# Merging two mixer branches and projecting out in one stage of 512-token blocks, with paired filter spectra and two DMA queues in the long convolutions

## Chip, cores and metric

The kernel runs on one core of one Trainium2 chip. The metric is the device time of one execution in microseconds (us); lower is better. Arithmetic is in float32; large products are split into a rounded high part and the rest (`hi`, `lo`), and three TensorE matmuls make one exact enough product. Engines are named as in the profile: PE (TensorE matmuls), PEld (its weight loads), DVE (VectorE), ACT (ScalarE), POOL (GpSimd), SP (SyncE).

## The reference

One layer over 2048 latent tokens and 256 context tokens of width 1024. After a modulated norm and one input projection, a Mamba-2 branch gives `y_m`, and a Hyena branch gives `y_h` by two rounds of long convolutions. What the changed stages compute is this, with the convolution done by FFT of 4096 points:

```
def bidir_long_conv(u, h_fwd, h_bwd):
    k = jnp.concatenate([h_fwd[:1] + h_bwd[:1], h_fwd[1:], jnp.zeros_like(h_fwd[:1]), jnp.flip(h_bwd[1:], axis=0)], axis=0)
    u_f, k_f = jnp.fft.rfft(u, n=2 * seqlen, axis=1), jnp.fft.rfft(k, n=2 * seqlen, axis=0)
    return jnp.fft.irfft(u_f * k_f[None], n=2 * seqlen, axis=1)[:, :seqlen]

for o, gate in enumerate((x1, x2)):                      # hyena_mixer
    z = gate * (bidir_long_conv(z, filt[:, 0, o], filt[:, 1, o]) + h_bias[o] * z)

ym = gated_group_rmsnorm(y_m, m_z, m_norm_w)             # mixer_output
yh = y_h * silu(h_gate)
merged = sigmoid(g_m) * (ym @ w_branch_m) + sigmoid(g_h) * (yh @ w_branch_h)
x = x + gate * (merged @ w_out)                          # gate: 1024 values from c, then a final rmsnorm
```

## The kernel before

The program is a row of phases, each a block in which every engine runs its own list of instructions, written out by hand and tied by semaphores. Nothing crosses from one phase into the next. Between phases, tensors lie in HBM, channels in rows and tokens in columns (`u_s`, `z2_s`, `hg_s`, `g_s`, `ym_s`, `mix_s`). The profile cuts digits off names, so `z2_s` reads `z_s` there.

**Long convolutions** (`phase_long_convs`, tiles `conv_...`). Four blocks of 256 channels, two orders each, are eight convolutions, in the order of the list `convs`. One convolution has a forward transform (`first`, from the tile `x`), then 32 planes: a matmul `forward`, DVE's product `prod` with the plane of the filter's spectrum (`spec`, 256 KB, L1078), two matmuls `inverse` (L995, L996). Then come `turn` (L963) and `last` (L973), and DVE multiplies by the gate `gin` into `x` (L1056), in four chunks of two products. PE does the transform of the next convolution and the turn of this one in one loop. All DMAs of the phase are on SP in one list: the spectra of a plane in two halves (L908, L910), through four slots; three gate chunks at planes 24, 26 and 28; at plane 4 after an order-1 convolution the store of `z2_s`, at plane 20 a new `x` (L890). SP works them off in this order, and a wait in one holds all behind it.

**Step sizes** (`phase_step_sizes`, `dt_...`) among other things computes the 1024 values of the output gate, repeated over 128 partitions, as 16 matmuls of 512 columns (L1128).

**Merge** (`phase_merge`, `mg_...`). Eight blocks of 256 tokens. Both branches' weights (16 slabs of 512 KB, one for each 128 output channels) are loaded once, split by ACT (high part) and by POOL and DVE in turn (low part), and stay. For each block and branch PE makes eight output tiles of 24 matmuls. DVE multiplies a tile by its gate, POOL adds the two branches, ACT stores to `mix_s`. The Mamba branch comes first, its group norm (squares, sums over partitions by PE, root, reciprocal) is done a block ahead.

**Output** (`phase_output`, `out_...`). `w_out` is loaded, scaled by the gate (DVE, L2066), split by ACT and POOL. Then come 16 tiles of 128 tokens: `mix_s` is loaded back and split, PE makes 2 by 24 matmuls of 512 columns with the tokens in rows, DVE adds the residual, and the norm and the store follow.

## Time and profile before

| | |
|---|---|
| time, 3 runs | 4273.19, 4275.51 (median), 4277.01 us |
| profiled execution | 4276.4 us, span 4274.6 us |
| mean granted clock of TensorE | 0.938 of full speed |
| busy | PE 3708.5, DVE 1663.0, ACT 1162.1, POOL 915.8 us |
| long convolutions | about 2224 to 2967 us of the span |
| merge and output | 3603 us to the end |

Busy time is a share of the whole span; each stage has its own limit, so the windows and the waits of a stage say more than the totals. PE's busy time includes matmuls that run at the lower clock. A wait is put down to what came last.

### The profile page before, as it was taken

Reading aid. Unit: us, or ns where it says so; the run is one execution under the profiler, and the core shown is the slowest. Engines: PE = TensorE matmul, PEld = TensorE weight load, DVE = VectorE, ACT = ScalarE, POOL = GpSimd, SP = SyncE. Lnnn points to the kernel's source line nnn. Section 1 sums busy time; section 2 is a strip of 40 time slices with the busy share of each in tenths; the row PEclk is TensorE's granted clock in tenths of the full one; section 3 lists DMA queues with packets and bytes.
Section 4 is the critical chain, followed back from the end, with each engine's and each line's share of the span. In section 5 each row is a group of like instructions: output and inputs, shape, how many; then the busy total and the mean of one; then the engine's idle time right before and its main releaser. Section 6 shows DMA issues by size and latency. Waiting matters only on the chain. (4 is left out here: it accounts for less than half of the span.)

```text
span 4274.6 us, 49330 instructions
## 1 busy us (share of the span) xinstructions
PE 3708.5 (87%) x18426; PEld 3067.7 (72%) x18426; DVE 1663.0 (39%) x1979; ACT 1162.1 (27%) x2308; POOL 915.8 (21%) x449
## 2 busy tenths in 40 slices
PE   6599999999999999967989978996456886799879
PEld 2588888888888888846977766764445775699867
DVE  6600443004333400045435443443176765455332
ACT  4311111111011111123764433442103552211022
POOL 0311222112222222110000000000056662433241
PEclk8799999999999999988999999998688998899989
DMA  6411111111111111179995665445785443443343
GB/s 244 154 59 74 70 67 69 74 74 73 64 69 74 74 74 74 54 283 298 293 247 140 146 143 138 114 122 156 256 307 200 155 159 128 148 137 128 110 141 123
DMA packets 595897, 588.97 MB, mean 138 GB/s; under 512 B 285627, under 2 KB 534619, under 8 KB 583387
## 3 DMA queue, kind: packets, MB, share of 16 engines
q1 hardware_dynamic: 515853, 421.13, 33.7%
q10 hardware_dynamic: 79920, 166.22, 10.0%
q8 instruction: 74, 1.21, 0.1%
q14 instruction: 50, 0.41, 0.0%
HBM read 375.84 MB, written 211.42 MB: 137 GB/s over the span
## 5 line engine op out<-in xcount | busy, mean ns | idle before, releaser
L563 PE MATMUL pl_bank<-hl_hi,pl_w_hi 128*128 128x512 f32 x2336 | 923.0, 395 | 17.1 <-POOL pl_w_lo L548 17.1
L564 PE MATMUL pl_bank<-hl_lo,pl_w_hi 128*128 128x512 f32 x2336 | 922.6, 395 | 0.0
L565 PE MATMUL pl_bank<-hl_hi,pl_w_lo 128*128 128x512 f32 x2336 | 922.6, 395 | 0.0
L563 PEld LDWEIGHTS pl_bank<-hl_hi,pl_w_hi 128*128 128x128 f32 x2336 | 440.8, 189 | 120.0 <-issue 17.3
L565 PEld LDWEIGHTS pl_bank<-hl_hi,pl_w_lo 128*128 128x128 f32 x2336 | 440.8, 189 | 103.1
L564 PEld LDWEIGHTS pl_bank<-hl_lo,pl_w_hi 128*128 128x128 f32 x2336 | 440.9, 189 | 102.9
L622 DVE TENSOR_SCALAR pl_acc<-pl_raw,pl_taps 128x2048 f32<-128x2048 f32 x40 | 83.8, 2094 | 930.2 <-ACT pl_raw L587 930.2
L545 POOL TENSOR_TENSOR pl_w_hi<-pl_w,pl_zero 128x1024 fp32r<-128x1024 f32 x73 | 138.3, 1894 | 1246.2 <-PE pl_bank L565 1242.0
L1338 POOL TENSOR_TENSOR st_faded<-st_state,ssd_whole 128x1024 f32<-128x1024 f32 x36 | 82.7, 2306 | 1209.0 <-DVE st_state L1365 1153.0
L1078 DVE TENSOR_TENSOR conv_prod<-conv_bank,conv_spec 128x512 f32<-128x512 f32 x256 | 175.3, 690 | 246.8 <-DMA conv_spec<-spec_s 208.1
L587 ACT ACTIVATE pl_raw<-pl_bank 128x512 f32<-128x512 f32 x160 | 91.7, 598 | 630.5 <-PE pl_bank L565 383.4
L587 ACT ACTIVATE pl_res<-pl_bank 128x512 f32<-128x512 f32 x132 | 78.9, 599 | 633.6 <-PE pl_bank L565 632.9
L1044 ACT COPY conv_v<-conv_bank 128x256 f32<-128x256 f32 x256 | 154.1, 602 | 310.0 <-PE conv_bank L996 310.0
L995 PE MATMUL conv_bank<-conv_prod,tab_wi 128*128 128x256 f32 x512 | 167.0, 409 | 77.3 <-DVE conv_prod L1078 76.5
L548 POOL TENSOR_TENSOR pl_w_lo<-pl_w,pl_w_hi 128x1024 fp32r<-128x1024 f32 x73 | 209.7, 2873 | 5.7
L1762 PE MATMUL mg_bank<-mg_m_hi,mg_w_hi 128*128 128x256 f32 x512 | 146.6, 286 | 44.5 <-DVE mg_mix L1927 27.4
L995 PEld LDWEIGHTS conv_bank<-conv_prod,tab_wi 128*128 128x128 f32 x512 | 96.8, 199 | 110.1 <-DVE conv_prod L1078 97.7
L624 DVE SCALAR_TENSOR_TENSOR pl_acc<-pl_raw,pl_taps,pl_acc 128x2048 f32<-128x2048 f32 x40 | 170.6, 4266 | 5.7 <-DVE pl_acc L622 0.2
L996 PE MATMUL conv_bank<-conv_prod,tab_wj 128*128 128x256 f32 x512 | 160.4, 396 | 0.0
L824 DVE COPY spec_y<-spec_bank 64x256 f32<-64x256 f32 x256 | 109.4, 427 | 124.0 <-PE spec_bank L798 121.9
L985 PE MATMUL conv_bank<-conv_y,tab_wf 128*128 128x256 f32 x512 | 154.1, 388 | 1.1 <-DVE conv_y L1018 1.1
L798 PEld LDWEIGHTS spec_bank<-tab_fk,spec_xin 128*128 128x128 f32 x1024 | 134.4, 195 | 25.2 <-DMA spec_xin<-kern_s 19.5
(224 smaller groups left out, 6748.3 us busy)
## 6 DMA issues: line engine op xcount, KB each, us to landing
conv_spec<-spec_s SPq DMA_DIRECT2D x504, 128.0 KB, 2.9
pl_w<-in_w_rec SPq DMA_DIRECT2D x73, 512.0 KB, 3.4
kern_s<-taps_res SPq DMA_DIRECT2D x16, 2048.0 KB, 7.0
spec_xin<-kern_s SPq DMA_DIRECT2D x64, 512.0 KB, 5.4
spec_s<-spec_res ACTq DMA_DIRECT2D x128, 256.0 KB, 3.9
st_xb<-tok_s SPq DMA_DIRECT2D x36, 768.0 KB, 6.9
u_s<-pl_res ACTq DMA_DIRECT2D x24, 1024.0 KB, 3.8
xbc_s<-pl_res ACTq DMA_DIRECT2D x16, 1024.0 KB, 3.8
```

What stands on the lines that cost most here:

```text
L548: nc.gpsimd.tensor_tensor(w_lo[:, q, :], w[:, q, 0:D], w_hi[:, q, :].bitcast(F32), ALU.subtract).then_inc(s_lo, 1)
L563: pe.matmul(out, w_hi[:, q, m], h_hi[:, k, r], start=(k == 0), stop=False)
L564: pe.matmul(out, w_hi[:, q, m], h_lo[:, k, r], start=False, stop=False)
L565: mm = pe.matmul(out, w_lo[:, q, m], h_hi[:, k, r], start=False, stop=(k == KT - 1))
L587: nc.scalar.activation(dst, bank[b][:, 0:BW], func).then_inc(s_ev, 1)
L624: nc.vector.scalar_tensor_tensor(out=acc[:], in0=raw[:, q, 0:T], scalar=w0, in1=acc[:], op0=ALU.mult, op1=ALU.add).then_inc(s_tap, 1)
L985: pe.matmul(bank[ubank[k % 4]][:, 0:CB], wf[:, k, :], y[:, k, :], start=True, stop=True).then_inc(s_u, 1)
L995: pe.matmul(out, wi[:, k, :], prod[:, n % 4, 0, :], start=True, stop=False)
L996: pe.matmul(out, wj[:, k, :], prod[:, n % 4, 1, :], start=False, stop=True).then_inc(s_v, 1)
L1044: nc.scalar.copy(v[:, :, k], bank[2 + k % 2][:, 0:CB]).then_inc(s_vm, 1)
L1078: nc.vector.tensor_tensor(prod[:, n % 4], bank[ubank[k % 4]][:, None, 0:CB].to_broadcast([P, 2, CB]), spec[:, n % SLOT], ALU.mult).then_in ...
L1762: pe.matmul(o, w_hi[:, n, m], hi[:, k, :], start=(k == 0), stop=False)
```

## The change

Four things change.

1. The long convolutions' spectra are loaded in pairs of planes: 256 KB a transfer, four slots of two planes. SP issues nothing else. The loads of `x` and of the gates and the stores of `z2_s` go to POOL's queue, in a list of their own, the store in four chunks.
2. The output gate is computed as one column for each 128 channels (`keep["gcol"]`), not repeated over partitions.
3. Merge and output become one phase (`phase_merge_output`, tiles `mo_...`) over four blocks of 512 tokens. In each block three branches of eight tiles follow: H (Hyena), M (Mamba), O (output projection). Each tile has 24 matmuls of 512 columns with channels in rows. The weight slab of every tile is loaded and split anew, through three slots. The scaling by the gate and the residual come after the O tile (`yT`); then PE turns `yT` by transposes into tokens in rows (`tok`, a single tile of two banks), four turns a block, each followed by the final norm and the store.
4. `mix_s` and the phase boundary between the two are gone.

In what follows a line of "..." stands where lines of the diff are left out, among them most that it removes; those are in the functions printed above.

```diff
-        spec = ph.sb("spec", [P, SLOT, 2, CB])
+        spec = ph.sb("spec", [P, SLOT, 2, 2, CB])
...
+            for j, (blk, o) in enumerate(convs):
+                for h in range(NPL // 2):
+                    n = NPL // 2 * j + h
+                    if n >= SLOT:
+                        sp.wait_ge(s_p, 2 * (n - SLOT) + 2)
+                    s = spec_v[o * NBK + blk, h]
+                    to = spec[:, n % SLOT].rearrange("p k a n -> p (k a) n")
+                    sem = s_k[n % SLOT]
+                    sp.dma_start(to[0:NA], s).then_inc(sem, 16)
+                    if h:
+                        sp.dma_start(to[NA:P], s).then_inc(sem, 16)
+                    else:
+                        sp.dma_start(to[NA + 1:P], s[1:NA]).then_inc(sem, 16)
+                        sp.dma_start(to[NA:NA + 1, 0], s[0:1, 1]).then_inc(sem, 16)
+                        sp.dma_start(to[NA:NA + 1, 1:4], s[0:1, 1:4]).then_inc(sem, 16)
+        @block.gpsimd
+        def _(pool):
+            def load_x(blk, c):
+                pool.dma_start(x[:, blk % 2, 16 * c:16 * (c + 1), :], u_v[0][blk, :, 16 * c:16 * (c + 1), :]
+                               ).then_inc(s_x[blk % 2][c], 16)
             def load_gate(j, c):
                 n = 4 * j + c
                 if n >= 3:
-                    sp.wait_ge(s_gate, 2 * (n - 3) + 2)
...
+                    pool.wait_ge(s_gate, 2 * (n - 3) + 2)
+                pool.dma_start(gin[:, n % 3], u_v[1 + convs[j][1]][convs[j][0], :, 16 * c:16 * (c + 1), :]
+                               ).then_inc(s_g[n % 3], 16)
+            for blk in range(2):
+                for c in range(4):
+                    load_x(blk, c)
+            for j, (blk, o) in enumerate(convs):
+                if o == 1:
+                    for c in range(4):
+                        load_gate(j, c)
+                    for c in range(4):
+                        pool.wait_ge(s_gate, 8 * j + 2 * c + 2)
+                        pool.dma_start(z2_v[blk, :, 16 * c:16 * (c + 1), :], x[:, blk % 2, 16 * c:16 * (c + 1), :]
+                                       ).then_inc(s_st, 16)
+                    if blk < 2:
+                        pool.wait_ge(s_st, 64 * (blk + 1))
+                        for c in range(4):
+                            load_x(blk + 2, c)
                 else:
...
+                    for c in range(4):
+                        load_gate(j, c)
+            pool.wait_ge(s_st, 256)
...
                         dve.wait_ge(s_u, n + 1)
-                        dve.wait_ge(s_k[n % SLOT], 32 * (n // SLOT + 1) + (32 * (j + 1) if k % SLOT == 0 else 0))
+                        if k % 2 == 0:
+                            h = n // 2
+                            dve.wait_ge(s_k[h % SLOT], 32 * (h // SLOT + 1) + (32 * (j + 1) if h % SLOT == 0 else 0))
...
-                                                spec[:, n % SLOT], ALU.mult).then_inc(s_p, 1)
+                                                spec[:, n // 2 % SLOT, k % 2], ALU.mult).then_inc(s_p, 1)
...
+            for m in range(KT):
+                if m % 4 == 0:
+                    pe.wait_ge(s_aw[m // 4], 16)
                 for k in range(KT):
+                    mm = pe.matmul(sums[4][:, 2 * m:2 * m + 2], aw[:, m // 4, k, m % 4 * P:(m % 4 + 1) * P],
+                                   keep["silu"][:, k, :], start=(k == 0), stop=(k == KT - 1))
+            mm.then_inc(s_gate, 1)
...
+def phase_merge_output(nc, t, keep, ym_s, z2_s, hg_s, gates_s, out):
+    BW = 512
     NB = SEQ // BW
+    NS = 3 * KT * NB
+    H, M, O = 0, 1, 2
+    par = keep["par"]
     with ExitStack() as ctx:
...
+        w = ph.sb("w", [P, 3, D])
+        w_hi, w_lo = ph.sb("w_hi", [P, 3, D], F32R), ph.sb("w_lo", [P, 3, D], F32R)
+        hi, lo = ph.sb("hi", [P, 2, KT, BW], F32R), ph.sb("lo", [P, 2, KT, BW], F32R)
+        zin = ph.sb("zin", [P, 2, 2, BW])
...
+        item = lambda b, br, k: KT * (3 * b + br) + k
+        def steps():
+            for b in range(NB):
+                for br in range(3):
+                    for j in range(KT):
+                        yield item(b, br, j), b, br, j
+        def rest(b, j):
+            if b:
+                return [j]
+            return [] if j < 4 else [2 * j - 8, 2 * j - 7]
         @block.sync
         def _(sp):
+            def load_w(s):
+                if s >= 3:
+                    sp.wait_ge(s_wlo, s - 2)
+                sp.dma_start(w[:, s % 3, :], t["w_br"][s % (3 * KT)]).then_inc(s_w[s % 3], 16)
+            def load_z(b, k):
+                n = KT * b + k
+                if n >= 2:
+                    sp.wait_ge(s_lo, item((n - 2) // KT, H, (n - 2) % KT) + 1)
+                sp.dma_start(zin[:, n % 2, 0, :], z2_v[:, k, cols(b)]).then_inc(s_z[n % 2], 16)
+                sp.dma_start(zin[:, n % 2, 1, :], hg_v[:, k, cols(b)]).then_inc(s_z[n % 2], 16)
+            def load_g(b, br, k):
+                n = 2 * KT * b + KT * br + k
+                if n >= 4:
+                    m = n - 4
+                    sp.wait_ge(s_ev, item(m // (2 * KT), m // KT % 2, m % KT) + 1)
+                sp.dma_start(gin[:, n % 4, :], g_v[1 - br, :, k, cols(b)]).then_inc(s_g[n % 4], 16)
+            def load_x(b, k):
+                n = KT * b + k
+                if n >= 4:
+                    sp.wait_ge(s_ev, item((n - 4) // KT, O, (n - 4) % KT) + 1)
+                sp.dma_start(xin[:, n % 4, :], x_v[:, k, cols(b)]).then_inc(s_x[n % 4], 16)
+            def load_ym(b):
+                if b:
+                    sp.wait_ge(s_lo, item(b - 1, M, KT - 1) + 1)
+                for a in range(4):
+                    sp.dma_start(ym[:, 2 * a:2 * a + 2], ym_v[:, 2 * a:2 * a + 2, cols(b)]).then_inc(s_ym[a], 16)
+            load_z(0, 0)
+            load_w(0)
+            load_z(0, 1)
+            load_w(1)
+            for k in range(2, KT):
+                load_z(0, k)
+            load_w(2)
+            load_ym(0)
+            sp.dma_start(ident[:], t["ident"]).then_inc(s_fw, 16)
+            sp.dma_start(fw[:], t["final_norm_w"].to_broadcast([P, D])).then_inc(s_fw, 16)
+            load_g(0, H, 0)
+            load_g(0, H, 1)
+            for s, b, br, j in steps():
+                if br == M and j == 0 and b + 1 < NB:
+                    load_ym(b + 1)
+                if s + 3 < NS:
+                    load_w(s + 3)
+                if s + 2 < NS:
+                    b2, br2, j2 = (s + 2) // (3 * KT), (s + 2) // KT % 3, (s + 2) % KT
+                    if br2 == O:
+                        load_x(b2, j2)
+                        if b2 + 1 < NB:
+                            load_z(b2 + 1, j2)
+                    else:
+                        load_g(b2, br2, j2)
...
+            def low(s):
+                pool.wait_ge(s_whi, s + 1)
+                nc.gpsimd.tensor_tensor(w_lo[:, s % 3, :], w[:, s % 3, :], w_hi[:, s % 3, :].bitcast(F32),
                                         ALU.subtract).then_inc(s_wlo, 1)
...
         @block.tensor
         def _(pe):
+            def tile(s, b, br, j):
+                pe.wait_ge(s_wlo, s + 1)
+                if s >= 4:
+                    pe.wait_ge(s_ev, s - 3)
+                q, slot = s % 3, (3 * b + br) % 2
+                for k in range(KT):
+                    if j == 0:
+                        pe.wait_ge(s_lo, item(b, br, k) + 1)
+                    m = slice(k * P, (k + 1) * P)
+                    pe.matmul(bank[s % 4][:], w_hi[:, q, m], hi[:, slot, k, :], start=(k == 0), stop=False)
+                    pe.matmul(bank[s % 4][:], w_hi[:, q, m], lo[:, slot, k, :], start=False, stop=False)
+                    mm = pe.matmul(bank[s % 4][:], w_lo[:, q, m], hi[:, slot, k, :], start=False, stop=(k == KT - 1))
                 mm.then_inc(s_mm, 1)
...
+            def turn(b, q):
+                n = 4 * b + q
+                pe.wait_ge(s_ev, item(b, O, KT - 1) + 1)
+                if n:
+                    pe.wait_ge(s_res, n)
+                for k in range(KT):
+                    mm = pe.transpose(tok[:, k // 4, k % 4 * P:(k % 4 + 1) * P], yT[:, k, q * P:(q + 1) * P], ident[:])
+                mm.then_inc(s_t, 1)
+            pe.wait_ge(s_one, 1)
+            pe.wait_ge(s_fw, 32)
+            for s, b, br, j in steps():
+                tile(s, b, br, j)
+                if b == 0 and br == H and j in (0, 1):
+                    sums(0, 2 * j)
+                    sums(0, 2 * j + 1)
+                if br == O and j in (1, 2) and b + 1 < NB:
+                    sums(b + 1, 2 * j - 2)
+                    sums(b + 1, 2 * j - 1)
+                if br == H and b and 1 <= j <= 4:
+                    turn(b - 1, j - 1)
+            for q in range(4):
+                turn(NB - 1, q)
         @block.scalar
         def _(act):
+            def weights(s):
+                act.wait_ge(s_w[s % 3], 16 * (s // 3 + 1))
+                if s >= 3:
+                    act.wait_ge(s_mm, s - 2)
+                nc.scalar.activation(w_hi[:, s % 3, :], w[:, s % 3, :], ACT.Copy).then_inc(s_whi, 1)
...
+            for s, b, br, j in steps():
+                if br == H:
+                    if b == 0 and j in (1, 2):
+                        mean(0, 2 * j - 2)
+                        mean(0, 2 * j - 1)
+                    if b and 2 <= j <= 5:
+                        finish(b - 1, j - 2)
+                    for k in rest(b, j):
+                        if b == 0 and k % 2 == 0:
+                            inverse(0, k // 2)
+                        m_value(b, k)
+                    gates(s, b, br, j, mixed[:, j, :]).then_inc(s_ev, 1)
+                    for k in rest(b, j):
+                        low(b, M, k)
+                elif br == M:
+                    gates(s, b, br, j, part[:, j % 2, :]).then_inc(s_ev, 1)
+                    if j:
+                        low(b, O, j - 1)
+                    dve.wait_ge(s_ev, s + 1)
+                    nc.vector.tensor_tensor(mixed[:, j, :], mixed[:, j, :], part[:, j % 2, :], ALU.add).then_inc(s_val, 1)
+                    if j == KT - 1:
+                        low(b, O, j)
+                else:
+                    if b + 1 < NB:
+                        if j in (2, 3):
+                            mean(b + 1, 2 * j - 4)
+                            mean(b + 1, 2 * j - 3)
+                        if j >= 4:
+                            inverse(b + 1, j - 4)
+                        h_value(b + 1, j)
+                    n = KT * b + j
+                    dve.wait_ge(s_mm, s + 1)
+                    dve.wait_ge(s_x[n % 4], 16 * (n // 4 + 1))
+                    if b and j == 0:
+                        dve.wait_ge(s_t, 4 * b)
+                    nc.vector.scalar_tensor_tensor(out=yT[:, j, :], in0=bank[s % 4][:], scalar=keep["gcol"][:, j:j + 1],
+                                                   in1=xin[:, n % 4, :], op0=ALU.mult, op1=ALU.add).then_inc(s_ev, 1)
+                    if b + 1 < NB:
+                        low(b + 1, H, j)
+            for q in range(4):
+                finish(NB - 1, q)
```

How the lists of DMAs change, at three places. The first is SP in the middle of the first convolution: planes from the 24th on, before.

```order
L908 DMA conv_spec<-spec_s 64x2x256
L910 DMA conv_spec<-spec_s 64x2x256
L897 DMA conv_gin<-u_s 128x16x64
L908 DMA conv_spec<-spec_s 64x2x256
L910 DMA conv_spec<-spec_s 64x2x256
```

The same queue of the changed kernel, at the stage's start (the first two planes have small transfers of their own):

```order
L896 DMA conv_spec<-spec_s 64x4x256
L900 DMA conv_spec<-spec_s 63x4x256
L901 DMA conv_spec<-spec_s 1x256
L902 DMA conv_spec<-spec_s 1x3x256
L896 DMA conv_spec<-spec_s 64x4x256
L898 DMA conv_spec<-spec_s 64x4x256
```

No gate load stands between spectra now; the pair of halves covers two planes. The second place is POOL's queue in the same stage, which had no instruction there before. This is its whole list; `x4` is four in a row.

```order
L907 DMA conv_x<-u_s 128x16x64 x8
L914 DMA conv_gin<-u_s 128x16x64 x12
L926 DMA z2_s<-conv_x 128x16x64 x4
L907 DMA conv_x<-u_s 128x16x64 x4
L914 DMA conv_gin<-u_s 128x16x64 x4
L926 DMA z2_s<-conv_x 128x16x64 x4
L907 DMA conv_x<-u_s 128x16x64 x4
L914 DMA conv_gin<-u_s 128x16x64 x12
L926 DMA z2_s<-conv_x 128x16x64 x4
L914 DMA conv_gin<-u_s 128x16x64 x4
L926 DMA z2_s<-conv_x 128x16x64 x4
```

All 64 transfers of `x`, gates and `z2_s` moved here; after the third and the fourth convolution the stores and the loads of a new `x` stand ahead of the next gates. The third place is SP at the start of the last stage. Before, in the merge:

```order
L1690 DMA mg_ym<-ym_s 128x4x256 x2
L1708 DMA mg_mix<-in_w_br 128x1024 x2
L1694 DMA mg_z2<-z2_s 128x4x256 x2
L1699 DMA mg_hg<-hg_s 128x2x256 x2
L1708 DMA mg_gates<-in_w_br 128x1024 x2
```

Now, behind seven pairs of `zin` loads (the last of them is shown), which are two deep:

```order
L1705 DMA mo_zin<-z2_s 128x512
L1706 DMA mo_zin<-hg_s 128x512
L1699 DMA mo_w<-in_w_br 128x1024
L1725 DMA mo_ym<-ym_s 128x2x512 x4
L1735 DMA mo_ident<-in_ident 128x128
L1736 DMA mo_fw<-in_final_norm_w 128x1024
L1713 DMA mo_gin<-g_s 128x512 x2
L1699 DMA mo_w<-in_w_br 128x1024
```

The branch that is computed first is the other one, so `ym` moved behind `z2_s`; the identity and the norm weights, which only the end of a block needs, are waited for by PE ahead of its first tile.

## Rows read from the trace of the kernel before

**Rows 1.** Windows of four stages: PE, PEld, DVE, ACT, POOL busy; clock; DMA share; GB/s.

```profile
2228.00:2957.00 729.00, 645.23 (x2816) 496.24 (x2816) 328.20 (x576) 318.89 (x640) 0.00 (x0) 0.96 0.57 135
...
3638.00:4050.00 412.00, 383.96 (x3128) 382.07 (x3128) 200.11 (x252) 72.17 (x106) 143.59 (x115) 0.96 0.40 130
...
4050.00:4090.00 40.00, 0.34 (x1) 0.35 (x2) 22.14 (x8) 10.35 (x10) 27.79 (x11) 0.55 0.54 184
...
4090.00:4267.00 177.00, 176.52 (x768) 145.54 (x767) 42.80 (x61) 35.15 (x59) 35.34 (x15) 0.99 0.38 128
```

**Rows 2.** The waits from 2228 to 2957: us, times, longest.

```profile
DVE conv_prod L1078 <- DMA conv_spec<-spec_s: 208.1, 170, 11.1
...
PE conv_bank L995 <- DVE conv_prod L1078: 76.5, 30, 8.8
```

**Rows 3.** The timeline of the first convolution, SP and PE: start, us, what.

```profile
2223.96 16.11 SPq L890 DMA_DIRECT2D conv_x<-u_s  x8
...
2228.21 4.34 PE L951 MATMUL conv_bank<-tab_fx,conv_x 128*128 128x256 f32 x12 [10.54 <-DMA conv_x<-u_s]
...
2247.80 1.53 PE L985 MATMUL conv_bank<-conv_y,tab_wf 128*128 128x256 f32 x6 [1.05 <-DVE conv_y L1018]
...
2277.74 1.61 SPq L908 DMA_DIRECT2D conv_spec<-spec_s  x1
```

**Rows 4.** The timeline of PE after the first z2 store.

```profile
2513.89 1.22 PE L995 MATMUL conv_bank<-conv_prod,tab_wi 128*128 128x256 f32 x2 [8.19 <-DVE conv_prod L1078]
```

**Rows 5.** The waits from 3602 to 4275.

```profile
PE mg_bank L1762 <- DVE mg_mix L1927: 27.4, 1, 27.4
...
PE out_bank L2023 <- POOL out_m_lo L2007: 40.3, 1, 40.3
```

**Rows 6.** The line of the x loads: issue ns, min/median/max, and landing.

```profile
L890 SPq DMA_DIRECT2D conv_x<-u_s x16: 372/2186/3646, 2224.0 to 2637.5; - x16
...
DMA to landing us min/median/max: 4.2/7.5/8.9
```

**Rows 7.** The timeline of DVE, first gate product of convolutions 0 and 1.

```profile
2303.83 0.69 DVE L1056 TENSOR_TENSOR conv_x<-conv_bank,conv_gin 128x512 f32<-128x512 f32 x1 [1.36 <-PE conv_bank L973]
...
2386.57 0.69 DVE L1056 TENSOR_TENSOR conv_x<-conv_bank,conv_gin 128x512 f32<-128x512 f32 x1 [1.36 <-PE conv_bank L973]
```

**Rows 8.** The timeline of PE in the step sizes, the output gate.

```profile
2982.32 15.59 PE L1128 MATMUL dt_sum<-dt_aw,dt_silu_rep 128*128 128x512 f32 x32 [7.50 <-DMA dt_aw<-in_ada_w]
```

**Rows 9.** The timeline of PE, four transposes.

```profile
2298.80 0.60 PE L963 MATMUL conv_bank<-tab_ident,conv_v 128*128 128x128 f32 x4
```

**Rows 10.** The windows of the projection and the output, 100 us each.

```profile
500.00:600.00 100.00, 100.00 (x432) 81.05 (x432) 42.09 (x15) 19.21 (x22) 23.58 (x9) 1.00 0.18 69
...
4120.00:4220.00 100.00, 100.00 (x443) 82.81 (x442) 25.42 (x36) 22.75 (x37) 23.21 (x10) 1.00 0.44 147
```

**Rows 11.** The groups of the merge: busy us, mean ns.

```profile
L1884 DVE RECIPROCAL mg_ms<-mg_ms 128x1024 f32<-128x1024 f32 x8 | 52.3, 6543 | 1.1 <-ACT mg_ms L1790 1.1
...
L1809 ACT ACTIVATE mg_w_hi<-mg_gates 128x1024 fp32r<-128x1024 f32 x8 | 8.3, 1054 | 2.9 <-DMA mg_gates<-in_w_br 2.9
...
L1853 POOL TENSOR_TENSOR mg_w_lo<-mg_gates,mg_w_hi 128x1024 fp32r<-128x1024 f32 x4 | 11.4, 2845 | 3.5 <-ACT mg_w_hi L1809 3.5
```

**Rows 12.** The timeline of the merge's start, SP and PE.

```profile
3607.47 0.92 SPq L1690 DMA_DIRECT2D mg_ym<-ym_s  x2
...
3637.96 0.58 PE L1762 MATMUL mg_bank<-mg_m_hi,mg_w_hi 128*128 128x256 f32 x1 [17.04 <-POOL mg_w_lo L1853]
```

**Rows 13.** The timeline of the end.

```profile
4266.56 1.22 DVE L2071 TENSOR_TENSOR out_y<-out_x,out_bank 128x1024 f32<-128x1024 f32 x1 [6.53 <-PE out_bank L2025]
...
4270.93 0.35 ACTq L2049 DMA_DIRECT2D out<-out_res  x1
```

**Rows 14.** The windows with gate loads and of the transforms behind.

```profile
2283.00:2289.00 6.00, 3.03 (x12) 2.12 (x12) 2.07 (x3) 1.20 (x2) 0.00 (x0) 1.00 1.18 227
...
2300.00:2310.00 10.00, 10.00 (x50) 7.30 (x49) 5.65 (x12) 6.49 (x16) 0.00 (x0) 1.00 0.01 2
```

More of the change, by code:

```diff
@@ L1974, in phase_output @@
-        block = ctx.enter_context(nc.Block())
-        def tiles(eng, body):
-            with eng.Fori(0, NT // 2) as i:
-                for q in range(2):
-                    body(2 * i + q, i, q)
+        ones, ident = ph.sb("ones", [P, P]), ph.sb("ident", [P, P])
+        bank = [ph.ps(f"bank{i}", [P, BW]) for i in range(4)]
+        ssq = [ph.ps(f"ssq{i}", [P, BW]) for i in range(2)]
+        tok = ph.ps("tok", [P, 2, BW])
+        s_w, s_whi, s_wlo, s_mm, s_ev = ph.sems("w", 3), ph.sem("whi"), ph.sem("wlo"), ph.sem("mm"), ph.sem("ev")
@@ new lines, in phase_merge_output @@
+        s_val, s_hi, s_lo, s_part = ph.sem("val"), ph.sem("hi_done"), ph.sem("lo_done"), ph.sem("part_done")
+        s_ym, s_z, s_g, s_x = ph.sems("ym_in", 4), ph.sems("z_in", 2), ph.sems("g_in", 4), ph.sems("x_in", 4)
+        s_sq, s_add, s_ss, s_ms, s_root, s_rec = (ph.sem(n) for n in ("sq_done", "add", "ss_done", "ms_done", "root", "rec"))
+        s_one, s_t, s_sq2, s_ms2, s_root2, s_rec2, s_res = (ph.sem(n) for n in (
+            "one", "turn", "sq2", "ms2", "root2", "rec2", "res_done"))
@@ new lines, in sums @@
+            def sums(b, g):
+                n = GROUPS * b + g
+                pe.wait_ge(s_add, n + 1)
+                if n >= 2:
+                    pe.wait_ge(s_ms, n - 1)
+                pe.matmul(ssq[g % 2][:], ones[:], ms[:, g, :], start=True, stop=True).then_inc(s_ss, 1)
+            def turn(b, q):
[6 more added lines that the diff above has]
+                mm.then_inc(s_t, 1)
@@ new lines, in store @@
+            def store(b, q):
+                n = 4 * b + q
+                act.wait_ge(s_res, n + 1)
+                act.dma_start(out[n * P:(n + 1) * P, :], res[:, n % 2, :]).then_inc(s_st[n % 2], 16)
+            for k in range(KT):
+                high(0, H, k)
+                if k in (1, 3):
+                    weights(k // 2)
+            for k in range(KT):
+                square(0, k)
+            for s, b, br, j in steps():
+                if s + 2 < NS:
+                    weights(s + 2)
+                if br == H:
+                    if b == 0 and j == 3:
+                        root(0)
+                    if b and 2 <= j <= 5:
+                        norm(b - 1, j - 2)
+                    for k in rest(b, j):
+                        high(b, M, k)
+                    if b and 3 <= j <= 6:
+                        store(b - 1, j - 3)
+                elif br == M:
+                    high(b, O, j)
+                    if b + 1 < NB:
+                        square(b + 1, j)
+                elif b + 1 < NB:
+                    if j == 4:
+                        root(b + 1)
+                    high(b + 1, H, j)
```

541 lines of the change are left out of this document (117 added, 424 removed).

## The prediction

> **What bounds the kernel now.** I read it stage by stage, because the change touches three stages and leaves the others alone. The busy times by window come first [rows 1]: in the long convolutions PE is busy for 645 of 729 us, in the merge for 384 of 412, between merge and output for 0.3 of 40, in the output for 176.5 of 177. So PE sets the pace wherever it has work, and what can be won is its idle time or its own instructions.
>
> The waits of the convolution stage [rows 2] say whose idle time it is: DVE's product with the spectra waits 208 us for the spectra's DMA, and PE's inverse transform waits 76.5 us in 30 pieces for DVE. The reader should see that these are one stall, and that the queue's order makes it. SP holds gate loads, the z2 store and x loads between the spectra: a spectrum behind a gate load took 1.61 us to issue [rows 3], and PE stood still for 8.19 us after the z2 store [rows 4].
>
> In the last two stages PE idles twice: 27.4 us while the second branch's weights are loaded and split, and 40.3 us while the output weights are scaled and split [rows 5].
>
> The sum is made against the profiled execution, 4276.4 us (span 4274.6 and 1.8 around it); the median of the runs is 4275.5, 0.9 lower. Less than 0.2% (8.6 us) cannot be told from no change.
>
> **Long convolutions, what goes.** SP keeps only spectra, in pairs: half as many issues of 256 KB instead of 128 KB. At worst a pair's two transfers cost twice what one spectrum's did, and the pace is as now; at best half. Taken away is the order: -76.5 us [rows 2].
>
> **Long convolutions, what comes.** All 64 transfers of x, gates and z2 (512 KB each, in rows of 256 bytes) go to POOL, which issues no DMA in the trace of before. So the time G from one to the next on POOL is unknown, and much hangs on it. From below, SP issued eight of the same transfers in 16.11 us [rows 3], 2.0 each; I take 2.2, the median of one issue [rows 6]. From above, 8.9 us, the slowest landing of one [rows 6]: then nothing overlaps. No row is near enough to choose by; I take the middle, G = 5.5.
>
> Start: now the first x load is issued at 2223.96, PE starts at 2228.21 and has used four chunks at 2247.80: 23.8 us, 4.9 a chunk [rows 3]. After it the fourth chunk lands at 4G + 2.2 (the quickest landing of 4.2 less 2.0 of issue [rows 6]) and takes 4.9: 29.1 us with G = 5.5, so +5. With 2.2: 0. With 8.9: +19.
>
> Period: where convolutions 2 and 3 end, POOL does in order, from the first product of a gate to the gate that the next convolution needs first: a gate load, four stores, a wait of about 5 us for their landing, four x loads, a gate load, and its landing of about 4: 10G + 9. From one convolution's first product to the next one's are 82.7 us [rows 7], about 78 without stalls. So up to G = 6.9 this costs nothing; beyond it, 10 us for each us of G, twice.
>
> Contention: after each of those two convolutions eight transfers (17.6 us at 2.2) run beside the spectra, which are eight planes ahead in their four pair slots. A plane lasts about 1.3 us of the stage (the period less its transform), so 10.3 us are covered; 7.3 is the most each can cost, 0 the least, since the DMA engines have a mean share of 0.57 here [rows 1]. I take 4 each: +8.
>
> End: the last stores follow one another at G, and one z2 store of 2 MB goes: -4 with 2.2, +4 with 5.5, +20 with 8.9.
>
> Sum: -76.5 + 5 + 8 + 4 = -60 (from -80 to +10).
>
> **Step sizes.** The output gate is computed as 64 matmuls of two columns instead of 16 of 512. Now these are 32 records in 15.6 us [rows 8]. After it they are 128 records, bound by their weight loads. Four 128x128 transposes, each with its own load, took 0.60 [rows 9], 0.15 each; half of that is my lower bound. 128 by 0.075 to 0.15 is 10 to 19 us. With a smaller copy behind it I take -3 (-6 to +3).
>
> **Merge and output.** PE's busy time now is 384.0 + 176.5 = 560.5 us [rows 1], 3072 matmuls of 256 columns, 768 of 512 and 28 sums of squares. After it there are 2304 of 512 columns. Their pitch is 0.2257 by the output stage (443 in 100 us) and 0.2315 by the projection (432), whose operands have the roles of the new ones [rows 10]; 0.229 gives 527.6 (520 to 533). The sums become 16 of 512 columns, at most 0.97 each by [rows 8]: 15. So -18.
>
> Both stalls go: -67.7 [rows 5], since weights are streamed, one slab of 512 KB for each output tile of 24 by 0.229 = 5.5 us. What hides it: ACT's half of the split takes 1.06 and POOL's 2.8 [rows 11], and they start two tiles ahead, when PE frees the slot: about 4.2 of 11 us. Without that cover each us over is paid in every one of 96 tiles.
>
> Sixteen turns of eight transposes come, at 0.11 to 0.15 each [rows 9]; twelve turns lie between tiles: +12.
>
> Start: now PE begins at 3637.96, 30.5 us after SP's first issue at 3607.47 [rows 12]. After it PE's first tile waits for the identity and the norm weights. SP issues them behind z loads that wait two by two for DVE's low parts (three round trips of about 6 us), a weight slab and 2 MB of ym (about 15 us with landing): 33.5, so +3.5.
>
> Block borders: in each of the last four tiles of O, DVE has a reciprocal of 3.27 (half of 6.54 [rows 11]) and three 512-wide operations of 0.69 (as those of [rows 7]): 5.34 us in a tile of 5.5, and it starts late behind ACT's root. The last low part comes some 3 us after the tile; PE wants it 4.8 us into the next. And with 2 MB of ym ahead of it in SP's queue, the fourth slab of branch M arrives about when it is wanted. Nothing to 25 us; I take +15, the slow clock of the first matmuls included.
>
> Tail: now 4266.56 to the end, 8.0 us [rows 13]. The four last turns share one PSUM tile, so each goes through turn, square, root, reciprocal and product before the next: 4270.93 - 4267.78 = 3.1 and the turn's 1.1, 4.2 by four, +0.7 ahead, 3.7 for the last store: 21. So +13.
>
> Sum: -18 - 67.7 + 12 + 3.5 + 15 + 13 = -42.
>
> **Total.** -60 - 3 - 42 = -105: 4171 us in the profiled execution, 4170.5 by the median; I say 4171. Its own range is 4145 (G = 2.2, a pitch of 0.2257) to 4200 (G = 6.9, late borders): chance 0.52.
>
> **Rivals.** First, POOL issues in 7 to 10 us. At 8.9: start +19, end +20, period 2 by 10 by 2.0 = +40, contention +8, against -76.5: +10. 4276 + 10 - 3 - 42 = 4241. For it speaks that no row has POOL issue at all, against it nothing but the same. 0.18.
>
> Second, slower than before: the same mechanism beyond its turning point. Each us beyond 8.9 costs 20 + 4 + 5 = 29, and 35 are left, so G = 10.1 decides. At G = 12 the time is 4330. The place is the convolution stage alone, PE waiting for gates and x. 0.15.
>
> Third, the spectra wait for the DMA engines and not for the queue's order. In a stretch with gate loads the share of the DMA engines is 1.18, in the transforms behind it 0.01 [rows 14]: full where PE waits. That the gates move to where it is 0.01 speaks for the gain; but x loads and stores still fall on the spectra, and their stalls of 8.2 at four places would stay: 33 of the 76.5. The stage then gives -27, and the time is 4204. The Trainium skill ("DMA: Bandwidth & Descriptors", section "Issuing engines are not separate DMA queues") says that starting transfers from several engines saves only the time of starting them, since the same 16 DMA engines carry all. The share of 1.18 agrees; by the rule alone it would be 4204. 0.08.
>
> Fourth, the new last stage is bound by its streams. 27 MB for each block of 132 us is 207 GB/s, and 238 in the tiles of O, against 130 in the merge now [rows 1]. Should the DMA engines give only 200, each of the 24 O tiles with loads for a next block takes 1.05 us longer, and late slabs double that: +25 to +50, about 4208. 0.07.
>
> **How the numbers follow.** Prediction 4171. The range is 4146 to 4280: 0.05 lies below (G at its lower bound and the rest good), 0.13 above (G over 10). Faster by over 0.2%: 0.52 + 0.18 + 0.08 + 0.07, less a little at the turning point: 0.83. Within 0.2%: 0.02. Slower: 0.15.
>
> **What would show it.** The spacing of POOL's issues in the convolutions: under 6.9 right, above it the price by the formula. PE's waits for the product with the spectra under 20 us in total. In the last stage: 3.5 us more to the first matmul, about 565 us to the last one, 21 behind it. A PE stall at the fourth tile of M or the first of H would be the borders, a stall in every tile the weights' split. What would make the prediction wrong above all is G.

## The result

The changed kernel takes 4172.9 us (median of 4 runs, 4165.82 to 4183.68), the kernel before 4274.8 in the same job (4273.19 to 4277.01): a ratio of 0.9764, 95% interval 0.9750 to 0.9779. 4171 was forecast. The profiled execution is the slowest of the four, 4183.7 us (span 4181.9); the stages below are read from it.

A stage is measured from its first DMA issue to that of the next; with the same code the changed convolutions took 676.3 to 683.2 us in six profiles, the changed last stage 615.9 to 619.3 in seven. These are the issues in the profile of the kernel before that don't stand ahead of the prediction ([rows 3, 12] have the other two):

```profile
2966.64 0.34 SPq L1106 DMA_DIRECT2D dt_raw<-dt_c  x1
...
3004.89 1.18 SPq L1234 DMA_DIRECT2D tok_in<-xbc_c  x2
```

And of the changed kernel, from the timelines of POOL and SP:

```profile
2231.60 9.32 POOL L907 DMA_DIRECT2D conv_x<-u_s  x8 [270.57 <-POOLq L63]
2242.95 1.15 POOL L914 DMA_DIRECT2D conv_gin<-u_s  x1 [2.03 <-issue]
...
2231.03 0.61 SPq L896 DMA_DIRECT2D conv_spec<-spec_s  x1
...
2910.68 0.33 SPq L1107 DMA_DIRECT2D dt_raw<-dt_c  x1
...
2961.43 1.16 SPq L1232 DMA_DIRECT2D tok_in<-xbc_c  x2
...
3562.72 0.34 SPq L1705 DMA_DIRECT2D mo_zin<-z_s  x1
```

| stage, us | before | after | change | forecast |
|---|---|---|---|---|
| up to the convolutions (not changed) | 2224.0 | 2231.0 | +7.1 | 0 |
| long convolutions | 742.7 | 679.6 | -63.1 | -60 |
| step sizes | 38.2 | 50.8 | +12.5 | -3 |
| the stages between (not changed) | 602.6 | 601.3 | -1.3 | 0 |
| merge and output | 667.1 | 619.2 | -47.9 | -42 |
| span | 4274.6 | 4181.9 | -92.7 | -105 |

The first row is no effect of the change. The projection, the same code in both, made 4305 matmuls from 500 to 1500 us in one profile and 4287 in the other, at a granted clock of 1.00 in both (last section).

The windows of the changed kernel, with the columns of [rows 1]: the convolutions, a pass over planes, a transform, the stretch after the first z2 stores, the output gate's matmuls, the last stage:

```profile
2238.89:2903.92 665.03, 630.82 (x2816) 493.95 (x2816) 327.18 (x576) 318.79 (x640) 65.21 (x57) 0.97 0.66 149
2345.00:2387.00 42.00, 42.00 (x200) 36.60 (x199) 21.24 (x33) 21.25 (x37) 0.00 (x0) 1.00 0.84 211
2318.00:2343.00 25.00, 24.91 (x112) 17.13 (x111) 14.14 (x29) 12.90 (x30) 3.81 (x4) 1.00 0.26 64
2501.00:2518.00 17.00, 13.42 (x63) 11.47 (x61) 5.53 (x8) 6.62 (x11) 8.00 (x7) 1.00 1.09 227
2924.00:2952.00 28.00, 27.45 (x129) 27.45 (x129) 8.95 (x14) 1.81 (x2) 0.00 (x0) 0.50 0.13 48
3600.00:4158.00 558.00, 552.94 (x2432) 450.88 (x2432) 328.15 (x340) 185.05 (x247) 249.03 (x107) 0.99 0.53 177
```

Read the last three columns (clock, share of the DMA engines, GB/s; the profile's share can come out over 1). A pass moves 211 GB/s, and by the view of DMA queues from 2345 to 2387 nearly all of it is SP's, that is spectra, 8.39 MB or 200 GB/s; POOL's 0.44 MB are the end of a gate load (packets, MB, share):

```profile
q1 hardware_dynamic: 8701, 8.39, 80.2%
q0 software_dynamic: 123, 0.44, 3.8%
```

A transform moves 64 GB/s, and where POOL's seven transfers (four of x, three of gates) come on top of a pass the engines are full at 227. The fifth line of the windows is the loser: PE is busy for 27.45 of 28 us, at half the clock. The waits of the convolution stage and the longest piece, beside those of [rows 2, 4], with a shorter piece behind it and the window in which the longest ends:

```profile
DVE conv_prod L1081 <- DMA conv_spec<-spec_s: 40.7, 13, 11.5
...
PE conv_bank L996 <- DVE conv_prod L1081: 30.9, 6, 9.1
...
2523.52 1.22 PE L996 MATMUL conv_bank<-conv_prod,tab_wi 128*128 128x256 f32 x2 [9.10 <-DVE conv_prod L1081]
...
2531.48 0.70 PE L996 MATMUL conv_bank<-conv_prod,tab_wi 128*128 128x256 f32 x2 [2.47 <-DVE conv_prod L1081]
...
2523.50:2526.00 2.50, 2.48 (x6) 2.03 (x7) 0.56 (x1) 0.36 (x1) 0.00 (x0) 0.50 1.07 238
```

76.5 us in 30 pieces became 30.9 in 6. PE's busy time for the same 2816 records fell as well, from 645.2 to 630.8. Behind the stall of 9.1 us the granted clock is 0.50 and a pair of matmuls takes 1.22 us; behind the one of 2.47 us it takes 0.70. There are fewer long stalls now, and the mean clock of the stage is 0.97 instead of 0.96.

Last, PE's timeline in the step sizes, at the start of the last stage and in the tail, which answers to [rows 8, 12, 13]:

```profile
2924.55 27.47 PE L1128 MATMUL dt_sum<-keep_silu,dt_aw 128*128 128x2 f32 x128 [5.09 <-DMA dt_aw<-in_ada_w]
...
3600.10 0.77 PE L1787 MATMUL mo_bank<-mo_hi,mo_w_hi 128*128 128x512 f32 x1 [42.72 <-DMA mo_fw<-in_final_norm_w]
...
4157.17 0.39 PE L1789 MATMUL mo_bank<-mo_hi,mo_w_lo 128*128 128x512 f32 x1
4158.40 1.09 PE L1805 MATMUL mo_tok<-mo_ident,mo_yT 128*128 128x128 f32 x8 [0.85 <-DVE mo_yT L1989]
4162.73 1.94 PE L1805 MATMUL mo_tok<-mo_ident,mo_yT 128*128 128x128 f32 x8 [3.24 <-DVE mo_res L1947]
```

### The profile page after: what moved, and what is told of

Read it like the earlier page. It is cut to its first block and busy times, and to the rows that moved or that the text cites. A ratio compares the mean times of both kernels' runs of the same rounds, so it can differ in the third digit from the quotient of the medians.

```text
span 4181.9 us, 45508 instructions
## 1 busy us (share of the span) xinstructions
PE 3715.1 (89%) x17082; PEld 3012.0 (72%) x17082; DVE 1723.6 (41%) x2008; ACT 1233.9 (30%) x2392; POOL 1033.8 (25%) x482
## 5 line engine op out<-in xcount | busy, mean ns | idle before, releaser
L1787 PE MATMUL mo_bank<-mo_hi,mo_w_hi 128*128 128x512 f32 x768 | 305.4, 398 | 47.2 <-DMA mo_fw<-in_final_norm_w 42.7
L1759 POOL TENSOR_TENSOR mo_w_lo<-mo_w,mo_w_hi 128x1024 fp32r<-128x1024 f32 x96 | 237.5, 2477 | 293.2 <-ACT mo_w_hi L1829 293.2
L1789 PE MATMUL mo_bank<-mo_hi,mo_w_lo 128*128 128x512 f32 x768 | 300.6, 391 | 0.0
L1788 PE MATMUL mo_bank<-mo_lo,mo_w_hi 128*128 128x512 f32 x768 | 300.6, 391 | 0.0
L1787 PEld LDWEIGHTS mo_bank<-mo_hi,mo_w_hi 128*128 128x128 f32 x768 | 145.2, 189 | 81.3 <-issue 45.0
L996 PE MATMUL conv_bank<-conv_prod,tab_wi 128*128 128x256 f32 x512 | 159.6, 394 | 31.5 <-DVE conv_prod L1081 30.9
L1788 PEld LDWEIGHTS mo_bank<-mo_lo,mo_w_hi 128*128 128x128 f32 x768 | 145.3, 189 | 31.6 <-issue 1.9
L1789 PEld LDWEIGHTS mo_bank<-mo_hi,mo_w_lo 128*128 128x128 f32 x768 | 145.0, 189 | 30.3
```

The costliest lines, as they stand in the source:

```text
L996: pe.matmul(out, wi[:, k, :], prod[:, n % 4, 0, :], start=True, stop=False)
L1759: nc.gpsimd.tensor_tensor(w_lo[:, s % 3, :], w[:, s % 3, :], w_hi[:, s % 3, :].bitcast(F32), ALU.subtract).then_inc(s_wlo, 1)
L1787: pe.matmul(bank[s % 4][:], w_hi[:, q, m], hi[:, slot, k, :], start=(k == 0), stop=False)
L1788: pe.matmul(bank[s % 4][:], w_hi[:, q, m], lo[:, slot, k, :], start=False, stop=False)
L1789: mm = pe.matmul(bank[s % 4][:], w_lo[:, q, m], hi[:, slot, k, :], start=False, stop=(k == KT - 1))
```

## The experiments

The first four take the convolution stage apart, the next four the step sizes and the two ends of the last stage; the last two follow from them. Stage lengths are from one profile each. Four kernels (the two output gates, the late wait, the tail) were run once, beside a run of 4285.1 us of the kernel before; since the runs of one kernel differ by up to 18 us, these four are read by their stages and not by their totals.

**The convolutions alone.** `phase_long_convs` of the changed kernel in the kernel before.

> The kernel before with the changed long convolutions alone (paired spectra on SP; x, gates and z2 on POOL). In the two profiles the stage from its first DMA issue to the first issue of the step sizes went from 742.7 us to 679.6. If the stages are independent, the stage here is again 680 (+-2) and the whole time is 63 below before, 4212 us (ratio 0.985), the other stages as before. Rival: a part of the 102 us comes from how the stages act on each other (clock, transfers that run over a border); then the whole moves by less than 55 or more than 71.

4211.4 us, ratio 0.985 (0.9829 to 0.9871); stage 683.2, the step sizes 38.6, the last stage 665.8. The stage is 1.2 us over the 682 that the expectation allowed, and the longest of the six profiles with the same code. Within that spread the stages are independent.

**Two queues with single planes.**

```diff
-                for h in range(NPL // 2):
+                for k in range(NPL):
+                    load_spec(j, k)
```

`load_spec` is that of the kernel before, on SP; everything else stays on POOL.

> The changed kernel, but the spectra are loaded plane by plane (128 KB an issue, four slots of one plane), SP still holding nothing else and POOL the rest. Theory order of the queue: what was won is that spectra no longer queue behind gates, x and z2, so nearly all of the 63 us stays: convolution stage 680 to 690 us. Rival issue time: SP needs 1.30 us for the two issues of a plane and PE 1.29 for a plane, so with single planes nothing can be caught up and the four slots cover half as much; then the stage goes back to 710 to 740 us.

Ratio 0.9828 (0.9804 to 0.9852), stage 699.9: between the two expectations.

**Pairs in one queue.**

```diff
         def _(sp):
...
+                    if k % 2 == 0:
+                        load_pair(j, k // 2)
+                    if j >= 1 and k == 4 and convs[j - 1][1] == 1:
...
```

Behind it z2, x and gates follow in SP's list as in the kernel before.

> The changed kernel, but x, gates and z2 stand in SP's list at their old places again, between paired spectra. Theory order of the queue: the stalls behind them come back, the stage is 725 to 745 us. Rival issue time: halved issues and slots twice as deep absorb a gate load of 0.6 to 1.7 us, only the z2 stores and x loads still stall (five stalls of 8 us); then the stage is 690 to 710 us.

Ratio 0.9857 (0.9837 to 0.9876), stage 718.0, again between the two expectations. PE's waits with single planes in two queues, and with pairs in one:

```profile
PE conv_bank L1000 <- DVE conv_prod L1083: 42.9, 18, 5.9
```

```profile
PE conv_bank L996 <- DVE conv_prod L1081: 58.4, 19, 7.3
```

From 742.7 us the pairs alone win 24.7, the second queue alone 42.8, both 63.1. Both theories hold for a part: the queue's order is the greater one, and the pairs are the other, on top of it. Which of the two things that pairs bring does it, slots twice as deep or half the issues, was not taken apart.

**The loads spread over the pass.**

```diff
+            def at(j, k):
+                pool.wait_ge(s_p, NPL * j + k)
...
                         for c in range(4):
+                            at(j + 1, 2 + 4 * c)
                             load_x(blk + 2, c)
```

The second x at the start and the first gate loads of a pass wait for planes in the same way.

> The changed kernel, but POOL's second x load at the start, and the x and first gate loads after the z2 stores, wait for the 2nd, 6th, 10th ... plane of the pass that they run beside (a wait for DVE's products, no byte more or less). PE's waits for the product are 30.9 us in 6 pieces now, each behind such a burst of up to 7 transfers of 512 KB. Theory burst: the DMA engines are full for the 17 us that a burst needs, spread over a pass of 42 us it fits beside the spectra; waits under 8 us, stage 645 to 655 us, the whole 25 to 33 us faster than the changed kernel. Rival: spectra are late for another reason (slots, SP's issues being slow by themselves); then the waits stay above 20 us and the stage at 672 to 680.

```profile
PE conv_bank L1006 <- DVE conv_prod L1091: 35.0, 13, 5.9
```

A miss. The waits broke into 13 shorter pieces and did not shrink; the stage is 685.0, no shorter, and the ratio 0.9769 (0.9747 to 0.9792), that of the changed kernel. So it is not the burst. What I had not looked at is the second line of the windows: the spectra alone take about 200 GB/s where 227 were moved with the engines full.

**The output gate with 128 columns.**

```diff
-                    mm = pe.matmul(sums[4][:, 2 * m:2 * m + 2], aw[...],
-                                   keep["silu"][:, k, :], ...)
+                    mm = pe.matmul(sums[4 + m // 4][:, m % 4 * P:(m % 4 + 1) * P], aw[...],
+                                   silu_rep[:, k, :], ...)
```

> The changed kernel, but the 64 matmuls of the output gate move 128 equal columns instead of 2 (same weights, same order, 64 times the columns). Now they take 27.5 us for 128 records (0.215 each) at a granted clock of 0.50 all the way; before, 32 records of 512 columns took 15.6 us at 0.89. Theory clock: matmuls of two columns never brought the clock up; with 128 columns it rises within a few us and the block takes 15 to 20 us. Rival weight loads: 128 loads of 128x128 in float32 cost 0.21 us each whatever is moved; then the block takes 27 us or more at a higher clock, or 0.50 stays.

4163.4 us in one run; window and timeline:

```profile
2918.00:2935.00 17.00, 16.36 (x129) 16.35 (x130) 8.96 (x14) 3.18 (x3) 0.00 (x0) 0.87 0.28 104
...
2918.64 16.29 PE L1131 MATMUL dt_sum<-dt_silu_rep,dt_aw 128*128 128x128 f32 x128 [3.79 <-DMA dt_aw<-in_ada_w]
```

64 times the columns in 16.3 us instead of 27.5, with the same 128 weight loads: the clock was 0.87 in the mean, and the loads had no price of 0.21 us of their own. (DVE repeats the vector over 128 columns ahead of it.) The eight mask matmuls behind it went from 4.19 us to 2.11. The stage is 36.4 us.

**The output gate as before, its column picked by DVE.** 16 matmuls of 512 columns, a product with the identity and a sum.

> The changed kernel with the 16 matmuls of 512 columns of before for the output gate (result equal in all partitions), and the column for each 128 channels picked out by DVE with a product with the identity and a sum over 128 columns. PE 15.6 us instead of 27.5; DVE's three or four operations add 3 us ahead of the last two mask matmuls. Stage of the step sizes from first issue to the next stage's first: 50.8 us in the changed kernel, 38.3 before; here 40 to 43. Rival: the matmuls' time was hidden behind DVE's chain anyway (it ended at 2934 in the changed kernel, the matmuls at 2952), then above 48.

4157.5 us in one run, stage 38.0 (40 to 43 expected, so the pick was cheaper than I thought), PE 16.7. The matmuls were on the path; the pick costs little.

**The late wait.**

```diff
             pe.wait_ge(s_one, 1)
-            pe.wait_ge(s_fw, 32)
...
             def turn(b, q):
+                if n == 0:
+                    pe.wait_ge(s_fw, 32)
```

> The changed kernel, but PE waits for the identity and the norm weights ahead of the first turn, not ahead of the first tile. In the changed kernel the first tile starts 37.4 us after the stage's first DMA issue, 30.5 in the kernel before. Theory: it was that wait alone; the first tile starts 26 to 29 us after the first issue, as soon as the first values are split, waits for the values of the 8th slab, and the last matmul ends 8 to 14 us earlier. Rival: the next late item, weight slab 2 or 3 behind 2 MB of ym in SP's queue, takes the place of the wait; then the last matmul moves by less than 4 us.

4168.5 us in one run. SP issues first at 3558.10, and then:

```profile
3570.37 0.77 PE L1787 MATMUL mo_bank<-mo_hi,mo_w_hi 128*128 128x512 f32 x1 [17.60 <-POOL mo_w_lo L1759]
```

12.3 us after the first issue, not 26 to 29 (PE waits for the slabs of values one by one, which I had forgotten), with 10.0 us of short waits for `lo` behind. The last stage is 608.6 us, 10.6 less, as expected. The wait for the norm weights caused the late start; of the 25 us by which PE now starts earlier, the short waits take 10.0, and 10.6 are left at the end.

**The tail with three PSUM tiles.** The last block's second and third turn go to the two pairs of tile banks; each square runs ahead of the root before it.

```diff
+        def toks(b, q):
+            return bank[:, 2 * q - 2:2 * q, :] if b == NB - 1 and q in (1, 2) else tok[:]
...
-                mm = pe.transpose(tok[:, ...
+                mm = pe.transpose(toks(b, q)[:, ...
```

> The changed kernel, but the turns of the last block use two more pairs of PSUM banks (the tiles' own four), so that they no longer wait for each other, and the squares run ahead of the roots. From the last output matmul to the span's end are 24.7 us in the changed kernel: 4.3 and three times 5.2, PE's transposes taking 1.94 us at half clock instead of 1.09. Theory: a chain through one PSUM tile; with three tiles DVE and ACT set 2.2 to 2.6 us a turn and the tail is 15 to 18 us. Rival: the store's landing and the chain of one turn dominate; tail above 21.

4162.2 us in one run, last stage 612.0, 7.2 less. The turns, where the second and third follow at once:

```profile
4145.60 1.09 PE L1810 MATMUL mo_tok<-mo_ident,mo_yT 128*128 128x128 f32 x8 [0.85 <-DVE mo_yT L2007]
4146.53 1.91 PE L1810 MATMUL mo_bank<-mo_ident,mo_yT 128*128 128x128 f32 x16
...
4150.85 1.06 PE L1810 MATMUL mo_tok<-mo_ident,mo_yT 128*128 128x128 f32 x8 [2.41 <-DVE mo_res L1965]
```

From the last output matmul's end (4144.75) to the span's end (4160.4) are 15.7 us, where the changed kernel has 24.3.

**The loads in the transforms.**

```diff
                     for c in range(4):
                         pool.wait_ge(s_gate, 8 * j + 2 * c + 2)
                         pool.dma_start(z2_v[...], x[...]).then_inc(s_st, 16)
+                        if c and j + 1 < NV:
+                            load_gate(j + 1, c - 1)
                     if blk < 2:
                         pool.wait_ge(s_st, 64 * (blk + 1))
                         for c in range(4):
+                            at(j + 1, (2, 12, 28, 28)[c])
                             load_x(blk + 2, c)
```

> The spread loads left 35 us of waits where 31 were, so the burst theory fell. New theory: bytes in a pass. In an undisturbed pass of 42 us the spectra alone move 209 to 211 GB/s, in the stalled stretches all together 220 to 227, in the transforms between passes 64 to 77: what else is put into a pass costs its bytes at 225 GB/s, wherever in the pass, less the 10 us that the four pair slots cover. Here, with the same bytes, the gates of the next convolution are loaded between the z2 stores, in the transform, two of four x chunks stay in the pass (1 MB, 4.7 us) and two go behind its 28th plane, at the start likewise. By this theory PE's waits for the product fall from 30.9 to under 8 us, the convolution stage from 679.6 (676 to 683 in the runs so far) to 640 to 652. Rival: it is the transfers' kind (rows of 256 bytes, two queues), and they slow the spectra for as long as they run, also in the prefetch of the four slots; then waits above 20 and the stage at 668 or more.

4144.1 us, ratio 0.9690 (0.9669 to 0.9712), stage 649.2. Waits, and windows of the stage and of 45 us of a pass and the transform behind it, with three x loads (issued from 2499.24 on):

```profile
PE conv_bank L1008 <- DVE conv_prod L1093: 11.1, 8, 1.8
```

```profile
2231.90:2865.00 633.10, 618.22 (x2815) 485.06 (x2816) 324.90 (x575) 318.96 (x640) 67.80 (x59) 1.00 0.72 156
2500.00:2545.00 45.00, 42.06 (x198) 33.89 (x197) 21.46 (x38) 23.45 (x46) 4.98 (x5) 1.00 0.96 189
```

The same bytes, a third of the waits (a little over the 8 expected), no piece over 1.8 us, and a clock of 1.00 in the stage, so PE's busy time fell again, to 618. Place decides, by what else moves at that time; the kind of transfer (rows of 256 bytes, POOL's queue) is the same and does not explain the stalls by itself.

**All together.** The convolutions of the last kernel, the wide gate, the late wait, the three PSUM tiles.

> Everything together: these loads in the transforms, 128 columns moved for the output gate (step sizes 36.4 us instead of 50.8), the late wait for the norm weights (last stage 10.6 us less) and the last turns in three PSUM pairs (7.2 less). If the four add, the stages are 646 + 36.4 + 600 + 601.4 behind a start of 2223 to 2231: 4112 us (4104 to 4122 with the start's two levels), 61 below the changed kernel. If the late wait and the tail interact, or the convolutions give nothing, 4125 to 4145.

4113.3 us (4107.98 to 4115.67), ratio 0.9614 (0.9593 to 0.9635), against 4112 expected. The stages are 649.9 (convolutions), 36.1 (step sizes), 600.7 (between, not changed) and 600.6 (last): the four changes add up. It is 60 us faster than the changed kernel.

## Why the prediction was right, and where it was not

The total came out right, 4171 against 4172.9, and several terms under it did not; that they made up for each other was luck. In the profiles, for which the sum was made, -105 was forecast and -92.7 measured: the changed stages give -98.5, and the start of the span, +7.1, is no effect of the change. Of the signs named ahead, POOL's spacing under 6.9 us came true, and waits for the product under 20 us did not (30.9).

**Stalls of the queue's order.** Right in kind: the wait of DVE for spectra was the stall, and taking the other transfers from SP wins most of it. The single-plane kernel shows that the pairs, which had no term in my sum, are worth 20 us on top. Forecast -76.5 in the stalls; measured -45.6.

**G.** The step that I took for the decisive one. POOL issues eight transfers in 9.32 us, 1.15 each: not 5.5, and under my lower bound of 2.2, which was SP's time for one such transfer. By the prediction's own terms so small a G would have given the stage -80 (it gave -63), so the total was saved by an offset: G too large, the stalls that stay too small.

**Contention**, mis-sized: +8 forecast. 30.9 us of stalls stayed, at the first pass, behind the two bursts of stores and loads (11.6 and 12.0 us) and near the end. I had read the DMA share as a mean over the stage, 0.57 [rows 1], while it is 0.84 in a pass and 0.26 in a transform. What comes in a pass costs its bytes: the seven transfers are 3.7 MB, 16 us at 227 GB/s, and the spread kernel shows that the place in the pass makes no difference. The size is not explained in full: the four slots cover 10 us by my estimate, so 6 us a burst should have been left, and it was nearly 12. The transforms' kernel takes the stalls to 11.1 by moving most of these bytes out of the passes.

So the third rival had the mechanism and a wrong size. It kept 33 us of stalls, and 30.9 were there; but it gave the stage -27. Its own -76.5 and +33 make -43.5; the rest of the way to -27 is +17 of start, contention and end taken over from the main sum, where the contention counts the same stalls twice, and the fall of PE's busy time is missing. The rule of the Trainium skill ("DMA: Bandwidth & Descriptors", section "Issuing engines are not separate DMA queues") says that a second issuing engine saves only the time of starting transfers, which it calls usually small. The trace agrees with it where the engines are full, share 1.09 at 227 GB/s. What a second queue saved here in all was not small, 42.8 us of the stage, because spectra no longer stood behind other transfers. How much of it is issue time on SP and how much the wait behind another transfer is not separated by any run; in the kernel before, SP's issue of the spectrum behind the first z2 store took 9.02 us:

```profile
2500.20 0.60 SPq L924 DMA_DIRECT2D z_s<-conv_x  x1
2500.85 9.02 SPq L908 DMA_DIRECT2D conv_spec<-spec_s  x1
```

**The clock behind stalls** was no term of the sum: -14.4, the fall of PE's busy time. **The start** was +3.6 (PE starts 7.9 us after the first issue, before 4.3), +5 forecast, but not by G, which would have made it 0: PE waits for the first x chunk, 7.3 us after POOL issues it at 2231.60. **The end** was -5.3 from the last product to the next stage (12.1 us before, 6.8 after), +4 forecast, with G again. -45.6 - 14.4 + 3.6 - 5.3 is -61.7; the rest is in waits too small for rows.

**Step sizes**, wrong in sign: -3 forecast (-6 to +3), +12.5 measured. My price of a matmul with its weight load was 0.075 to 0.15 from transposes at the full clock [rows 9]; it was 0.215 at half the clock. The trace of before had shown the clock at 0.50 in the short transposes just ahead, and I priced the matmuls as if it were 1.00. A window there, with the columns of [rows 1]:

```profile
2970.00:2982.00 12.00, 2.12 (x18) 1.99 (x18) 4.04 (x8) 4.16 (x5) 0.00 (x0) 0.50 0.92 322
```

The wide gate has a mean of 0.87 in the same place, with 128 columns.

**Merge and output**, -42 forecast, -47.9 measured. First to last matmul: 628.6 us before, 557.5 after, -71.1, where matmuls, stalls, turns and borders made -58.7. The borders were too dear: PE's waits for POOL's and DVE's low parts there are 4.5 us, in five pieces, not 15. The first matmuls at half the clock cost 2 more. The pitch was 0.2267 (a tile of 24 in 5.44 us), not 0.229: -5. The sums were as forecast, 1.72 us for two in the chain that ended last, 14 for all 16 against 15; a turn between tiles took 0.87, 10 for twelve against 12. These differences make about -16 where -12.4 was measured, so some 4 us stand in no row. The weight splits were hidden, as forecast, and the fourth rival (streams) did not come: 0.53 of the DMA engines and 177 GB/s in the stage. The start was +6.9 (37.4 us from first issue to first matmul), +3.5 forecast (my own 33.5 less 30.5 is 3.0), by the wait that was named. The tail was +16.3 (24.3 us), +13 forecast: the chain is as told, but three of the four turns run at half the clock, 1.94 us for 1.09.

The slower rival and that of a slow POOL fell with G.

## What to carry to other kernels

Before transfers are moved to another queue, look at the bytes of the stretch where they will land, not at the mean of the stage: a queue changes their order, and here they came near to free only where the DMA engines had idle time. Matmuls that save columns can cost time: here, where a stretch of them was all that PE did, 128 records took 16.3 us with 128 equal columns and 27.5 with 2. A wait at the head of an engine's program for something that is needed only at the end is worth a look: here it was 10.6 us.

## What the runs showed of the hardware

POOL issues a transfer of 512 KB in rows of 256 bytes in 1.15 us, at a share of the DMA engines of 1.09 (seven in 8.00 us from 2501 to 2518) as elsewhere (SP needed 2.0, and up to 3.6 [rows 6]). SP's issues do grow: in the changed kernel a half pair takes 0.6 us, and in the stretch of share 1.09

```profile
2511.81 5.42 SPq L896 DMA_DIRECT2D conv_spec<-spec_s  x1
```

The x loads landed after 7.5 us (median) in the kernel before; the view of DMA issues of the changed one (KB each, median us to landing) has:

```profile
conv_x<-u_s POOLq DMA_DIRECT2D x16, 512.0 KB, 13.2
```

PE at a busy share of 0.98 stayed at a granted clock of 0.50, the level of 1.2 GHz, for 28 us of two-column matmuls, after it had waited for DMA and done 18 small transposes; with 128 columns in the same place the mean was 0.87. 227 GB/s is what was moved with the engines full in the convolutions; the window in the step sizes above has 322 at a share of 0.92, with other transfers.

The projection, whose code is the same in all kernels here, ran at one of two paces with the clock at 1.00 in both: 4305 matmuls from 500 to 1500 us in eight of the twelve profiles, 4287 or 4288 in four (the changed kernel, the pairs in one queue, the late wait and the wide gate). That is 0.4%, about 7 us over the projection, the first row of the table at the top. What chooses the pace is open, and so is how much of the 18 us between the runs of one kernel it explains.
